# Streaming encoder step: two convolution first steps move from VectorE to ScalarE, and the opening of each feed-forward stage is issued in another order

## The reference, cut to what matters

```
def causal_dwconv(u, prev, w, b):
    L = u.shape[1]
    full = jnp.concatenate([prev, u], axis=1)
    out = b + sum(full[:, i:i + L] * w[i] for i in range(3))
    return out, full[:, -2:]

def conv_glu(h, prev, w_in, conv_w, conv_b, w_out):
    g, u = jnp.split(h @ w_in, [D_FF], axis=-1)      # D_FF = 2816 = 22 tiles of 128
    gc, new_prev = causal_dwconv(g, prev, conv_w, conv_b)
    return (gelu(gc) * u) @ w_out, new_prev
```

## Time and profile before

| | |
|---|---|
| Median of 3 runs | 2598.21 us |
| Lowest, highest | 2597.47, 2599.83 us |
| The profiled execution, its own time | 2597.79 us |
| Its span, first to last instruction | 2595.9 us |
| Mean granted TensorE clock | 0.998 |
| TensorE busy | 97% of the span |
| VectorE, ScalarE, GpSimd busy | 63%, 40%, 31% |

### The profile page before, as it was taken

How to read it: one execution, slowest core, us unless ns; L and a number is a source line. 1 busy time by engine, 2 the same in 40 slices (tenths; PEclk the granted TensorE clock), 3 DMA queues, 4 the chain that set the end, 5 groups by cost and what they waited for, 6 DMA issues and landing times.

```text
span 2595.9 us, 44346 instructions
## 1 busy us (share of the span) xinstructions
PE 2529.0 (97%) x18550; PEld 2450.4 (94%) x18550; DVE 1645.5 (63%) x2628; ACT 1050.6 (40%) x1727; POOL 796.1 (31%) x524
## 2 busy tenths in 40 slices
PE   8999999999999999999999999999999999999999
PEld 6999999999999999999998998989999999999999
DVE  6735353569766765774724886555697676658754
ACT  6433333364332333332436676444553233333312
POOL 5121212162444434002522124323434443440002
PEclk9999999999999999999999999999999999999999
DMA  3111111132323335452113445122122333336522
GB/s 111 36 37 35 37 35 37 35 104 74 116 92 114 102 99 200 132 166 83 55 41 112 145 154 170 56 99 75 62 80 94 114 108 105 111 129 203 166 79 81
DMA packets 229682, 252.26 MB, mean 97 GB/s; under 512 B 16849, under 2 KB 178271, under 8 KB 228591
## 3 DMA queue, kind: packets, MB, share of 16 engines
q1 hardware_dynamic: 227087, 247.36, 29.1%
q10 hardware_dynamic: 2400, 2.10, 0.3%
HBM read 173.54 MB, written 75.89 MB: 96 GB/s over the span
## 4 chain that ended last, share of the span: by engine, by line
PE 79%; DVE 12%; issue 4%; ACT 3%; DMA 1%; POOL 1%; SPq 0%; DVEq 0%; ACTq 0%; POOLq 0%
PE ps L898 13%; PE ps L900 13%; PE ps L899 13%; PE ps L346 9%; PE ps L348 8%; PE ps L347 8%; PE ps L2791 3%; PE ps L1688 1%; PE ps L2776 1%; PE ps L1675 1%; PE ps L1677 1%; PE ps L1676 1%; DVE hflat L491 1%; PE ps L1764 1%; PE ps L1747 1%
## 5 line engine op out<-in xcount | busy, mean ns | idle before, releaser
L1560 POOL TENSOR_TENSOR wlo<-wraw,whi 128x1024 fp32r<-128x1024 f32 x78 | 192.5, 2469 | 440.0 <-DVE s_raw L1251 440.0
L311 POOL TENSOR_TENSOR wlo<-wraw,whi 128x2048 fp32r<-128x2048 f32 (+1 forms) x21 | 94.3, 4492 | 591.2 <-ACT whi L304 561.7
L898 PE MATMUL ps<-hh,whi 128*128 128x264 f32 x928 | 264.8, 285 | 3.3 <-DVE hf L1328 2.3
L900 PE MATMUL ps<-hh,wlo 128*128 128x264 f32 x928 | 264.2, 285 | 0.0
L899 PE MATMUL ps<-hl,whi 128*128 128x264 f32 x928 | 264.1, 285 | 0.0
L346 PE MATMUL ps<-hh,whi 128*128 128x352 f32 x648 | 218.7, 338 | 0.6 <-ACT cqr L3126 0.3
L348 PE MATMUL ps<-hh,wlo 128*128 128x352 f32 x648 | 208.4, 322 | 0.0
L347 PE MATMUL ps<-hl,whi 128*128 128x352 f32 x648 | 208.1, 321 | 0.0
L590 DVE TENSOR_TENSOR xT<-xT,ps 128x352 f32<-128x352 f32 x288 | 147.3, 518 | 87.3 <-PE ps L348 86.1
L898 PEld LDWEIGHTS ps<-hh,whi 128*128 128x128 f32 x928 | 174.8, 188 | 4.4 <-DVE hf L1328 2.7
L1560 POOL TENSOR_TENSOR s_lo<-s_raw,s_hi 128x512 fp32r<-128x512 f32 x80 | 157.9, 1973 | 60.1 <-DVE wlo L1292 30.1
(11 more groups left out here) (461 smaller groups left out, 8680.3 us busy)
## 6 DMA issues: line engine op xcount, KB each, us to landing
wraw<-w_ffn_in SPq DMA_DIRECT2D x88, 512.0 KB, 3.8
s_a<-hf SPq DMA_DIRECT2D x44, 528.0 KB, 3.3
wraw<-w_ffn_out SPq DMA_DIRECT2D x44, 512.0 KB, 3.8
s_t<-h SPq DMA_DIRECT2D x16, 1056.0 KB, 4.5
hflat<-s_t SPq DMA_DIRECT2D x16, 1056.0 KB, 6.3
h<-s_a SPq DMA_DIRECT2D x12, 1056.0 KB, 5.6
wraw<-w_gla_in SPq DMA_DIRECT2D x24, 512.0 KB, 4.5
s_x<-xT SPq DMA_DIRECT2D x6, 1408.0 KB, 5.5
```

Of the source, the lines that this page charges most:

```text
L311: pool.tensor_tensor(lo[:, 0:cols], raw[:, 0:cols], hi[:, 0:cols].bitcast(F32), ALU.subtract).then_inc(S("w_lo"), 1)
L898: nc.tensor.matmul(out, w_[0], x_[0], start=first, stop=False, skip_group_check=True)
L900: last = nc.tensor.matmul(out, w_[1], x_[0], start=False, stop=(k == HK - 1), skip_group_check=True)
L1560: return pool.tensor_tensor(lo[:, cols], raw[:, cols], hi[:, cols].bitcast(F32), ALU.subtract)
```

## The change

ScalarE makes the first step of the convolutions of units 0 and 1 (new function `conv_base`, an activation `Identity` with the tap as its scale and the bias as its bias), and VectorE's TENSOR_SCALAR is left out there. ScalarE's list for units 2 and 3 is written out: snap 1 of unit 2 and snaps 0 and 1 of unit 3 stand ahead of the Gelus that were ahead of them, and snap 2 of unit 3 stays behind the high parts of unit 4's weights. On VectorE `up_left(2)` moves from within `conv(1)` to ahead of it, and the pair sums T1 and T3 of the first pair move from behind `s_sums(4)` to ahead of it. The counts of the semaphores `gate_taken` and `conv_step` are adapted. All of it happens once in each of the two layers.

```diff
+            def conv_base(f):
+                if f:
+                    act.wait_ge(S("summed"), cnt("summed", layer, f, 2))
+                    act.wait_ge(S("glu"), NF * layer + f)
+                else:
+                    act.wait_ge(S("gate_taken"), 4 * layer + 1)
+                cv = par[:, 1 + layer, :]
+                act.activation(fc[:, :], fg[f % 2][:, 2:2 + T], ACT.Identity,
+                               bias=cv[:, f + 3 * NF:f + 3 * NF + 1],
+                               scale=cv[:, f + 2 * NF:f + 2 * NF + 1]).then_inc(S("gate_taken"), 1)
...
             snap(1, 1)
+            conv_base(0)
             snap(1, 2)
             w_hi_sums(2)
-            for f in range(2, NF):
+            snap(2, 0)
+            snap(2, 1)
+            gelu(0)
+            w_hi_in(3)
+            conv_base(1)
+            w_hi_sums(3)
+            snap(2, 2)
+            snap(3, 0)
+            gelu(1)
+            snap(3, 1)
+            gelu(2)
+            w_hi_in(4)
+            w_hi_sums(4)
+            snap(3, 2)
+            for f in range(4, NF):
                 snap(f, 0)
-                gelu(f - 1 if f > 2 else 0)
+                gelu(f - 1)
                 if f < NF - 1:
                     w_hi_in(f + 1)
                     snap(f, 1)
                     w_hi_sums(f + 1)
                     snap(f, 2)
-                if f == 2:
-                    gelu(1)
...
                     dve.wait_ge(S("glu"), NF * layer + f)
+                if f < 2:
+                    dve.wait_ge(S("gate_taken"), 4 * layer + 3 + f)
+                    if f:
+                        dve.wait_ge(S("conv_step"), steps + 1)
                 else:
-                    dve.wait_ge(S("gate_taken"), 2 * layer + 1)
-                dve.tensor_scalar(fc[:, :], g[:, 2:2 + T], cv[:, f + 2 * NF:f + 2 * NF + 1],
-                                  cv[:, f + 3 * NF:f + 3 * NF + 1], ALU.mult, ALU.add).then_inc(S("conv_step"), 1)
-                dve.wait_ge(S("conv_step"), steps + 1)
+                    dve.tensor_scalar(fc[:, :], g[:, 2:2 + T], cv[:, f + 2 * NF:f + 2 * NF + 1],
+                                      cv[:, f + 3 * NF:f + 3 * NF + 1], ALU.mult, ALU.add).then_inc(S("conv_step"), 1)
+                    dve.wait_ge(S("conv_step"), steps + 1)
...
             up_right(2)
-            conv(1, lambda: (up_left(2), gate_right(2)))
+            up_left(2)
+            conv(1, lambda: gate_right(2))
             glu(1)
             conv(2)
             for f in range(3, NF):
                 gate_left(f)
                 glu(f - 1)
+                if f == 3:
+                    pair_sum(0, "T1")
+                    pair_sum(0, "T3")
                 if f < NF - 1:
                     s_sums(f + 1)
                 else:
                     block_lo("X11", 0)
                 pair = (f - 3) // 2 if f % 2 and f <= 2 * NT + 1 else None
-                if pair is not None:
+                if pair:
                     pair_sum(pair, "T1")
                     pair_sum(pair, "T3")
                 up_right(f)
```

More of the change, by code:

```diff
@@ L926, in p2 @@
                 if f == 1:
-                    pe.wait_ge(S("gate_taken"), 2 * layer + 1)
+                    pe.wait_ge(S("gate_taken"), 4 * layer + 1)
                 else:
@@ L961, in p3 @@
                 if f == 1:
-                    pe.wait_ge(S("gate_taken"), 2 * layer + 2)
+                    pe.wait_ge(S("gate_taken"), 4 * layer + 2)
                     pe.wait_ge(S("s_lo"), cnt("s_lo", layer, f, 2))
@@ L1350, in conv @@
                     dve.wait_ge(S("summed"), cnt("summed", layer, f, 4))
-                    dve.tensor_copy(s_[:, 2:2 + DEC], g[:, 2 + SEQ:2 + T])
+                    copied = dve.tensor_copy(s_[:, 2:2 + DEC], g[:, 2 + SEQ:2 + T])
+                    if f == 1:
+                        copied.then_inc(S("conv_step"), 1)
                     dve.wait_ge(S("glu"), NF * layer + f)
-                else:
-                    dve.wait_ge(S("gate_taken"), 2 * layer + 1)
-                dve.tensor_scalar(fc[:, :], g[:, 2:2 + T], cv[:, f + 2 * NF:f + 2 * NF + 1],
-                                  cv[:, f + 3 * NF:f + 3 * NF + 1], ALU.mult, ALU.add).then_inc(S("conv_step"), 1)
-                dve.wait_ge(S("conv_step"), steps + 1)
+                if f < 2:
+                    dve.wait_ge(S("gate_taken"), 4 * layer + 3 + f)
+                    if f:
+                        dve.wait_ge(S("conv_step"), steps + 1)
+                else:
+                    dve.tensor_scalar(fc[:, :], g[:, 2:2 + T], cv[:, f + 2 * NF:f + 2 * NF + 1],
+                                      cv[:, f + 3 * NF:f + 3 * NF + 1], ALU.mult, ALU.add).then_inc(S("conv_step"), 1)
+                    dve.wait_ge(S("conv_step"), steps + 1)
                 dve.scalar_tensor_tensor(fc[:, 0:SEQ], g[:, 1:1 + SEQ], cv[:, f + NF:f + NF + 1], fc[:, 0:SEQ],
-                                         ALU.mult, ALU.add).then_inc(S("conv_step"), 1)
+                                         ALU.mult, ALU.add).then_inc(S("conv_step"), 1 if f else 2)
                 dve.scalar_tensor_tensor(fc[:, SEQ:T], s_[:, 1:1 + DEC], cv[:, f + NF:f + NF + 1], fc[:, SEQ:T],
@@ L1375, in glu @@
                 if f == 0:
-                    dve.wait_ge(S("gate_taken"), 2 * layer + 2)
+                    dve.wait_ge(S("gate_taken"), 4 * layer + 2)
                 v = a_rows(f)
```

## The result

The changed kernel takes 2605.19 us (median of 19 runs, 2603.09 to 2608.96), the kernel before 2597.91 us (19 runs, 2594.22 to 2603.3): ratio 1.0027, 95% interval 1.0020 to 1.0033. It is slower by 7.3 us. The forecast was 2600.7 us and no measurable change, and its range ended at 2603.8 us, so both were wrong. The profiled execution took 2604.02 us, with a span of 2602.0.

The account below looks back on a forecast made before the run. TensorE, busy 97% of the span, was taken as the bound. P3 of unit 3 later by 1.1 us in layer 0 and 1.4 in layer 1 made 2598.2 + 2.5 = 2600.7 us, range 2596.6 to 2603.8.

Parts of the forecast that it names:

- Where to look: Only the start of P3 of unit 3 counts; waits at P2, P6, P7 go, one of some 4.6 us stands there.
- Gelu 0 with the table load: ScalarE, unit 2: load behind snap 1 is no longer hidden; `glu(0)` at 625.1 against 623.56, +1.6 us (layer 1 +1.8).
- Convolution 1 against GpSimd: `conv(1)`: VectorE and GpSimd wait for each other in turn; with snap 0 first, Gelu 1 starts at 641.5, +0.9 us.
- what would show it: List of expected trace signs: load position, `glu(0)` times, TensorE's waits, unit lengths, and VectorE instruction times in `conv(1)`.
- From `glu(2)` to P3 of unit 3: 9.2 us against 9.0, +0.2: contention saved by early T1 and T3 is paid again by `w_hi_sums(4)` in series.
- The sum behind P3: After P3 of unit 3 the delay carries through unchanged: +1.1 us in layer 0, +1.4 in layer 1, +2.5 in all.
- The slower rival of the prediction: `Identity` needs another table, so Gelu 1 pays 1.28 us more per layer: 2603.3 us; further or dearer loads 0.08.
- the estimate with the drain beside its sum: Table load at Gelu 0 also brings a drain on the path, 2 x 1.38 us more: +5.3 us, slower by just over 0.2%.
- the faster rivals: Load off the path, 2598.1 us (0.14); VectorE not held by GpSimd in `conv(1)`, 2596.6 (0.06); both, 2593.8 (0.05).

Follow-up runs that it names:

- e2_table: Changed kernel with the Gelu's table loaded early, between snap 1 of unit 1 and the first convolution step; ratio 1.0016 to the kernel before.
- f3_gelu0_first: Changed kernel with Gelu 0 ahead of snap 1 of unit 2 again; ratio 1.0014 to the kernel before.
- e1_fill: Changed kernel with 36 matmuls nobody reads between P4 and P3 of unit 3 in each layer; ratio 1.0019 to the kernel before.
- h1_before_late: Kernel before with the last high part of unit 4's weights written five times, so snap 2 of unit 3 comes late; ratio 1.0043 to the kernel before.
- h2_before_late_fill: h1_before_late with 36 matmuls nobody reads between P4 and P3 of unit 3; ratio 1.0024 to the kernel before.
- f5_pairs_back_fill: Changed kernel, T1 and T3 behind `s_sums(4)` again, plus 16 unread matmuls at P3 of unit 2 and 30 at P3 of unit 3; ratio 1.0006 to before.
- e3_snap: Changed kernel with snap 2 of unit 3 ahead of the high parts of unit 4's weights on ScalarE; ratio 0.9996 to the kernel before.
- f1_pairs_back: Changed kernel with the pair sums T1 and T3 behind `s_sums(4)` again; ratio 1.0024 to the kernel before.

## Why the prediction was wrong

Point by point, by its own steps:

- *Where to look.* Right. P3 of unit 3 decided. The waits at P2, P6 and P7 went, and the time did not follow them. The one wait of 4 to 5 us came in layer 0 (4.80); in layer 1 it was 3.10, since half clock in unit 2 had delayed TensorE's own work.
- *Gelu 0 with the table load.* Right to 0.1 us: `glu(0)` at 625.13 after the offset, forecast 625.1. e2_table and f3_gelu0_first show its price, 1.4 us for the load and 2.2 with the snap ahead of it.
- *Convolution 1 against GpSimd.* Right in the end, wrong on the way. The first SCALAR_TENSOR_TENSOR got no turn between GpSimd's two parts; the small copy ahead of it (1.72 us, 0.18 when alone) took that turn. Both orders lead to about the same end. Predicted 2.6 us for the SCALAR_TENSOR_TENSOR, measured 3.26; predicted over 2 for the small one, measured 0.24. This point of the list "what would show it" was wrong without touching the time.
- *From `glu(2)` to P3 of unit 3.* Predicted 9.2 us, measured 9.57 in layer 0 (649.96 to 659.53) and 9.23 in layer 1 (1965.32 to 1974.55). The difference is a gap of 0.46 us between `glu(2)` and T1 in layer 0. The profile puts it down to T1's wait for `glu(2)`, but the same two stand 0.10 apart in layer 1, so that dependency is not the whole cause, and the rest of it stays open. Together with 0.2 us before it, P3 came 1.7 us later than before in layer 0, and not 1.1; in layer 1 it was 1.55 for 1.4.
- *The sum behind P3.* **This step failed.** "Behind it, TensorE has no wait to take the delay up", and so a delay of 1.1 us was carried as 1.1 us. The prediction itself foresaw "one of some 4.6 us" at this place, gathered from four waits of up to 1.37 us, and priced it as if TensorE came back from it at full speed. It came back at half clock: P3 took 4.95 us in place of 3.0, so 2.0 us in layer 0; in layer 1 P3's first matmul to P1 of unit 4 took 4.54 us, 1.5 more. In that layer the wait of 2.24 us at P3 of unit 2 was also followed by a half-clock stretch (at 1950.7), which delayed TensorE's own work and was swallowed by the next wait.

In numbers: units 2 and 3 are longer by 3.7 and 3.1 us in the profiled execution. In layer 0 that is 1.7 of lateness and 2.0 of clock; in layer 1 1.55 and 1.5. Together 6.7 us: 3.3 of lateness, for which the prediction had 2.5, and 3.5 of clock, for which it had nothing. The spans of the two profiled executions differ by 6.1 us (2602.0 against 2595.9): besides the 6.7, the changed kernel reached unit 2 of layer 0 0.9 later, and was 0.4 shorter between the two places and 1.1 after the second. The medians differ by 7.3. What is left is within what one execution can differ from another: the kernel before has a spread of 9 us over its 19 runs.

The slower rival of the prediction, and the estimate with the drain beside its sum, had the right sign and the wrong cause: no second load, no drain. VectorE was held by GpSimd, as forecast (3.26 us), so the faster rivals fell as well.

The Trainium skill (TensorE: Matmul & The Clock Gate, Why this matters for your kernels) warns against idle gaps of TensorE between bursts of matmuls, since the clock falls back. It was this rule that spoke against the change, and the prediction did not weigh it. The runs agree: e1_fill, h1_before_late with h2_before_late_fill, and f5_pairs_back_fill all show full clock when the same wait is filled.

Left open: what decides whether a wait of about 2 us is followed by half clock. In the stretches of the profiled executions, each of the seven unfilled waits of 4.4 us or more was followed by it (layer 0 of the changed kernel, both layers of e2_table, f3_gelu0_first and h1_before_late). Of ten between 1.8 and 2.3 us five were: at P3 of unit 2 the same wait of 2.23 to 2.24 us was followed by half clock in layer 1 and not in layer 0 of the changed kernel, and the other way round in e3_snap. Of three between 2.9 and 3.1 us, all at P3 of unit 3 with half clock at P3 of unit 2 before them, one was. Open too is where the runs that were not profiled lose their time: the medians of f1_pairs_back and f5_pairs_back_fill lie 4.5 us apart, their profiled executions 1.7 us the other way.

## What to carry to other kernels

When several short waits of TensorE hang on one late chain, taking away the first ones without shortening the chain gathers them into one long wait at the last; and a wait of TensorE has two prices, its length and, if it is long enough to bring the clock down, what the matmuls behind it lose at 1.2 GHz. So look for the step whose start the chain sets, shorten the chain there, and price a wait that grows by rows at both clocks. Before moving a copy ahead of an activation, look whether that activation's table load used to hide in the wait that is being filled. And a step that is taken off a chain gains nothing if the chain then stands behind something put in series with it: here two weight copies of 2.35 us in front of one copy that TensorE waited for.

## What the runs showed of the hardware

A wait of TensorE of 4.4 to 4.8 us within dense matmul work was followed by 1.2 GHz in all seven cases that were profiled, one of about 2 us in five of ten; the spacing of 128x264 matmuls was 0.22 us in place of 0.12. Thirty-six matmuls with no use, issued into the wait, kept 2.4 GHz (h2_before_late_fill against h1_before_late) and saved 1.5 us at each place. They cost time where the wait turned out shorter than they are: layer 1 of e1_fill, P3 1.1 us later.

A VectorE copy of 32 columns took 1.72 us in place of 0.18 while GpSimd ran a subtraction, and ended when that ended (636.20 and 636.16). GpSimd's next instruction began at once, and the VectorE instruction of 1,024 columns behind the copy then took 3.26 us in place of 1.28. Layer 1 shows the same, 1.70 and 3.23.

A table load of ScalarE ran directly behind the instruction ahead of it and not at the end of the wait of its Gelu: at 616.79 for a Gelu at 622.44 in the kernel before. With a copy in between it stood on the path, and cost 1.4 us at P3 of unit 3 (e2_table).
